# Attention of a hybrid decoder block: row blocks of a head taken in the order 0, 3, 1, 2

## The reference, cut to what matters

```python
qh = jnp.concatenate([q_nope, q_pe], axis=-1) * (QK_DIM ** -0.5)     # 128 + 64 columns, 8 heads
q_blocks = qh.reshape(B, n_blk, Q_BLOCK, H, QK_DIM)...               # 4 blocks of 128 rows
def block(args):
    q_i, i = args
    s = jnp.einsum('bhqd,bhkd->bhqk', q_i, kh).astype(jnp.float32)
    s = jnp.where(kpos[None, :] <= qpos[:, None], s, NEG_INF)
    prob = jax.nn.softmax(s, axis=-1).astype(vh.dtype)
    return jnp.einsum('bhqk,bhkd->bhqd', prob, vh)
...
merged = jax.nn.sigmoid(gate_a) * y_a + jax.nn.sigmoid(gate_b) * y_b
x = x + merged @ w_o[l]
```

## Time and profile before

| what | value |
|---|---|
| median of three runs | 1158.05 us |
| span of the profiled execution, first to last instruction | 1155.5 us |
| TensorE busy | 1109.0 us, 96% of the span |
| VectorE busy | 854.7 us, 74% |
| ScalarE busy | 783.1 us, 68% |
| GpSimd busy | 413.2 us, 36% |
| the four steps of a head in attention, heads 1 to 6 | 7.46 to 8.77 us |

### The profile page before, as it was taken

The page is one execution under the profiler, slowest core; times in us unless marked ns, Lnnn a source line. Parts: engine busy times, 40 slices in busy tenths (PEclk is TensorE's granted clock), DMA queues, the critical chain, the costliest instruction groups (busy, mean ns, idle before and its releaser), DMA issues. The chain is left out here.

```text
span 1155.5 us, 17715 instructions
## 1 busy us (share of the span) xinstructions
PE 1109.0 (96%) x5459; PEld 909.9 (79%) x5459; DVE 854.7 (74%) x1211; ACT 783.1 (68%) x1266; POOL 413.2 (36%) x477
## 2 busy tenths in 40 slices
PE   7999999999899999999999999999999999999898
PEld 7888888788678886888888887777878878777677
DVE  3536534277664586999999988888899989899665
ACT  6644434367553335888888888788888888887562
POOL 1220000033473002455555553444555555454320
PEclk9999999999999999999999999999999999999999
DMA  6422322113203098999999999999999999999631
GB/s 241 146 73 82 136 73 75 38 60 101 100 2 128 37 367 311 379 322 358 383 388 385 384 386 377 362 359 361 369 362 371 366 365 379 366 369 364 173 123 73
DMA packets 71955, 291.61 MB, mean 252 GB/s; under 512 B 15139, under 2 KB 20550, under 8 KB 46950
## 3 DMA queue, kind: packets, MB, share of 16 engines
q1 hardware_dynamic: 52496, 254.13, 56.6%
q0 software_dynamic: 18768, 34.79, 11.9%
q10 hardware_dynamic: 646, 2.12, 0.5%
HBM read 284.61 MB, written 42.07 MB: 283 GB/s over the span
## 5 line engine op out<-in xcount | busy, mean ns | idle before, releaser
L1518 DVE TENSOR_TENSOR arena_r<-arena,win_r 128x1024 fp32r<-128x1024 f32 x252 | 292.1, 1220 | 51.7 <-ACT win_r L986 46.7
L986 ACT ACTIVATE win_r<-arena 128x1024 fp32r<-128x1024 f32 x252 | 246.2, 1056 | 57.8 <-DMA arena<-in_w_exp_up 53.4
L1929 PE MATMUL bank<-win_r,work_r 128*128 128x512 f32 x512 | 205.3, 401 | 19.6 <-DVE x_low_r L1477 19.1
L669 POOL DMA_INDIRECT moe_sum<-ya,sidx x64 | 121.0, 1890 | 252.4 <-ACT ya L1019 252.4
L1930 PE MATMUL bank<-win_r,x_low_r 128*128 128x512 f32 x512 | 199.4, 390 | 0.0
L1931 PE MATMUL bank<-arena_r,work_r 128*128 128x512 f32 x504 | 197.0, 391 | 0.0
L1492 DVE TENSOR_TENSOR arena_r<-arena,hT_r 128x1024 fp32r<-128x1024 f32 x128 | 150.5, 1218 | 0.0
L1929 PEld LDWEIGHTS bank<-win_r,work_r 128*128 128x128 f32 x512 | 96.3, 188 | 43.8 <-issue 25.9
L1663 PE MATMUL bank<-arena_r,hT_r 128*128 128x512 f32 (+2 forms) x320 | 121.8, 381 | 1.2 <-DVE win_r L1129 1.2
L1667 PE MATMUL bank<-win_r,hT_r 128*128 128x512 f32 (+2 forms) x320 | 120.4, 376 | 0.0
L1664 PE MATMUL bank<-arena_r 128*128 128x512 f32 (+2 forms) x320 | 120.4, 376 | 0.0
(11 more groups left out here) (290 smaller groups left out, 2173.3 us busy)
## 6 DMA issues: line engine op xcount, KB each, us to landing
arena<-in_w_exp_down SPq DMA_DIRECT2D x64, 1024.0 KB, 15.8
arena<-in_w_exp_gate SPq DMA_DIRECT2D x63, 1024.0 KB
arena<-in_w_exp_up SPq DMA_DIRECT2D x63, 1024.0 KB
win<-in_w_in SPq DMA_DIRECT2D x8, 2048.0 KB, 7.7
win<-in_w_o SPq DMA_DIRECT2D x2, 2048.0 KB, 7.9
arena<-in_w_ple_gate SPq DMA_DIRECT2D x2, 2048.0 KB, 24.5
arena<-moe_sum SPq DMA_DIRECT2D x8, 512.0 KB, 7.6
win<-in_mla_w_qb SPq DMA_DIRECT2D x4, 576.0 KB, 4.0
```

Source lines behind the costliest of these rows:

```text
L669: pool.indirect_dma_start(sums[j % 2], bass.IndirectOffsetOnAxis(sidx[j % 2][0:NS, 0:1], 0), yo[j % 2][0:NS], None, bounds_check=last_toke ...
L986: act.activation(gu_hi[n % 2][:, :, cols], raw[:, :, cols], ACT.Copy).then_inc(gu_hi_r, 1)
L1518: dve.tensor_tensor(low_[:, :, cols], raw[:, :, cols], gu_hi[n % 2][:, :, cols].bitcast(F32), ALU.subtract).then_inc(gu_lo_r, 1)
L1929: pe.matmul(b_, x_hi[:, k, :], w_hi, start=(k == 0), stop=False)
```

## The change

Row blocks of heads 0 to 6 are taken in the order 0, 3, 1, 2. The last head keeps 0, 1, 2, 3. All five instruction lists use the same new function for the row block of a pair, and nothing else is changed: buffers, semaphores, their counts, and the work placed by the step number stay.

```diff
+    BLOCK_ORDER = (0, 3, 1, 2)
+
+    def head_block(s):
+        h, at_ = divmod(s, NT)
+        return h, (at_ if h == H - 1 else BLOCK_ORDER[at_])
...
             for n in range(NA):
-                h, i = divmod(n, NT)
+                h, i = head_block(n)
                 pool.wait_ge(o_ready, n + 1)
...
                 if s < NA:
-                    i = s % NT
-                    W = (i + 1) * P
+                    W = (head_block(s)[1] + 1) * P
                     act.wait_ge(nm_ready, s + 1)
...
                 if s < NA:
-                    W = (s % NT + 1) * P
+                    W = (head_block(s)[1] + 1) * P
                     dve.wait_ge(s_done, s + 1)
...
                 if s < NA:
-                    h, i = divmod(s, NT)
+                    h, i = head_block(s)
                     W = (i + 1) * P
...
-                    for k in range(n % NT + 1):
+                    for k in range(head_block(n)[1] + 1):
                         last = pe.transpose(bank[4 + n % 2][:, tok(k)], probs[n % 2][:, tok(k)], ident[:, :])
```

More of the change, by code:

```diff
@@ L881, in _ @@
                     n = s - 1
-                    W = (n % NT + 1) * P
+                    W = (head_block(n)[1] + 1) * P
                     act.wait_ge(pt_done, n + 1)
```

## The result

The changed kernel takes 1166.42 us, the median of four runs (1165.50 to 1168.44), against 1157.57 us for the kernel before beside it (1156.11 to 1160.28): ratio 1.0074, 95% interval 1.0055 to 1.0092. A second set of runs of both on one chip gave 1.0057 (1.0038 to 1.0076). The forecast was 1165.2 us and the range 1161.3 to 1167.4.

A forecast was written before the change was run, and what follows sets the result against it. Attention was taken as bound by TensorE's list, 7.11 us of work plus 0.47 of waiting per 7.58 us head. Head-by-head changes summed to +7.15 us, which with the median gave 1165.2 us, range 1161.3 to 1167.4.

The forecast's parts named there:

- The bound: Attention heads: TensorE's list sets the time, 7.11 us of work and 0.47 of waiting in a 7.58 us head.
- (a): TensorE's wait at T4, the widest block's transposes: falls from 0.48 to 0.24 us, by itself worth 0.24 per head 1 to 6.
- (b): Rotary pieces now follow the widest block's exp4 on ScalarE: `rope_low` ready at 5.09 us of the head, ahead of max2.
- (c): `rope_low` on VectorE comes behind GpSimd's long subtraction and waits 0.75 us for it, within bounds 0 and 0.75.
- Rival 1: `rope_low` is not held by the subtraction, at most 0.22 us: total +4.0, 1162.1 us; chance 0.18.
- (d): Late max2 and exp2 delay the copy of T4's result; PV4 starts at 8.16 and ends the head at 9.05 us.
- The sum: Changes of heads 0 to 7 added up: heads 3 to 6 +5.68, head 7 -0.87, together +7.15 us.
- The carry to the end: Shared expert loads wait for attention's last addition, so attention's shift carries to the end of the kernel.
- Rival 3: Attention gets longer but the end does not move, as the expert stage waits for weights anyway: 1158.3 us; chance 0.09.
- Rival 2: Rotary pieces stay hidden and only the shorter T4 wait counts, so the kernel is faster: 1155.9 us; chance 0.05.

The follow-up runs named there:

- e3: Kernel before, order 0, 1, 2, 3 kept, with both rotary pieces moved earlier; ratio to the kernel before 0.9994.
- e2: Changed kernel with `rope_high` one step earlier and `rope_low` one step earlier, behind the row maximum; ratio to the kernel before 0.9976.
- e5: Changed kernel with only `rope_high` one step earlier, `rope_low` left ahead of max2; ratio to the kernel before 0.9983.
- e1: Changed kernel with GpSimd's w_o pieces one pair later, so a short rounding copy stands ahead of `rope_low`; ratio to the kernel before 1.0027.
- e8: Changed kernel with each GpSimd subtraction cut into two of 256 columns; ratio to the kernel before 1.0032.
- e4: Changed kernel with both rotary pieces moved earlier and the row blocks in order 0, 3, 2, 1; ratio to the kernel before 0.9993.

## Why the prediction was right, step by step

- **The bound.** Right. TensorE's groups cost the same in both kernels, PV4 apart, and what moved was waiting. e3 shows T4's chain as the period of the order of before, with the rotary pieces elsewhere. That these pieces cost nothing before holds for the steady heads; in heads 1 and 2 they cost 0.81 together, which the prediction did not see.
- **(a), T4's wait falling to 0.24.** Right, and seen twice: 323.45 to 323.69 in the changed kernel, 328.10 to 328.34 in e2.
- **(b), the rotary pieces behind exp4.** Right. In head 3, with t = 0 at 319.28, exp4 came at 3.58 (3.60 said), `rope_high` at 4.42 (4.44), `rope_low` at 5.07 (5.09). e5 shows that this place on ScalarE is the cause.
- **(c), `rope_low` held by the subtraction.** Right. The subtraction started at 4.68 (4.71 said), max2 at 6.53 (6.56). This was the part without a row of its own, bounded by 0 and 0.75; it was 0.73 (1.42 less 0.69). e1 and e8 show it by taking it away and by cutting it. Rival 1, with 0.22 of the hold left, would have been 3.2 us less; e1's attention, with 0.06 or nothing of it left, is 3.88 us less.
- **(d), PV4 as the end of the head.** Right in place, with two small errors that nearly cancel: PV4 began at 8.09 (8.16 said) and took 1.00 where 0.89 was taken. The longer time was in the earlier trace rows already: PV4 behind a wait has a record of 1.16, without one 1.06.
- **The sum.** Head by head against before: head 0 +0.12 (0.15 said), head 1 +1.19 (1.15), head 2 +0.95 (1.04), heads 3 to 6 +1.39, +1.48, +1.38, +1.49 (together 5.74, 5.68 said), head 7 -0.92 up to S3 (0.87). Together 7.08; 7.15 was said. The largest miss is head 2, by 0.09.
- **The carry to the end.** Right: the SyncE queue waits 7.1 us longer, and the ratios of the two sets are 8.6 and 6.6 us. Rival 3 falls. The measured median is 1.2 us above the forecast, and no stage of the change accounts for that: attention grew by 0.07 less than said, and the executions differ by about as much ahead of it.
- **Rival 2**, the gain of 2.1 us with the pieces hidden, did not happen. Once the pieces are moved (e2) the gain is 2.98 us in attention and 2.8 by the ratio. Heads 3 to 6 gain 1.09 of it and head 7 gains 0.93 (0.96 and 0.87 said). Most of what lies above the 2.1 is in heads 1 and 2, which gain 1.08 where 0.48 was taken.

## What to carry to other kernels

When the order of work is changed in a pipeline written by step number, read which side pieces are tied to the step and not to the size, and walk each engine's list once with the new neighbours: here the gain of the order was 2.4 us of attention, and the price of two small pieces left in place some 10 (66.25 against 56.19). Where two engines hold each other up, as VectorE and GpSimd do here, the question is who comes first: `rope_low` came 0.39 us too late and waited 0.73 for the other's instruction. Cut that instruction (e8) or move it (e1). A longer distance for the slowest chain helps only until the next chain is the slowest, so count all of them, with the engines' own queues.

## What the runs showed of the hardware

- The hold between a VectorE operation with two inputs in SBUF and a GpSimd subtraction or addition goes by instruction and in both directions: `rope_low` 1.42 and 1.29 us against 0.69 behind a 512-column subtraction, 0.88 and 0.75 behind a 256-column one, and the addition 0.95 against 0.46 when it came second by 0.05 us. The Trainium skill, SBUF — State Buffer, section "SBUF: two separate sides", says that the first one keeps the shared ports for its whole instruction; the trace agrees nearly. In head 3 `rope_low` was held 0.73 from 324.35, to 325.08, 0.15 before the recorded end of the subtraction at 325.23.
- A VectorE operation that reads one operand in PSUM and one of 128 columns in SBUF was not held: in e2, L1326 at 329.46 took its 0.35 inside a subtraction of GpSimd that ran from 329.26 to 330.54 (1.28 us, as without a meeting).
- TensorE's group PV4 takes some 0.10 us more when it begins behind a wait (1.00 in the changed kernel, e4 and e8 and 0.99 in e1, against 0.89 in the earlier trace rows and 0.90 in e2, from start to next start). Why is not shown.
